# RWKV-7 scan rounds on TensorE: waits on constants, turns inside 64x64 tiles, and a new order of the steps

## The chip, the cores and the metric

One core of one Trainium2 chip runs the kernel. The metric is the device time of one execution in microseconds. PE is TensorE, DVE is VectorE, ACT is ScalarE, POOL is GpSimd.

## The reference, cut to what matters

The program is a network of several layers over 256 context and 256 latent tokens of width 1024, in fp32. One of them is an RWKV-7 layer with 16 heads of 64 channels, and the change is inside its recurrence. For each head and direction (context first, then the latent tokens from the context's last state):

```python
def step(S, inp):                       # S is 64 x 64 for each head
    rt, wt, kt, vt, kkt, at = inp
    sa = jnp.einsum("bhvk,bhk->bhv", S, -kkt)
    S = S * wt[:, :, None, :] + sa[..., None] * (kkt * at)[:, :, None, :] + vt[..., None] * kt[:, :, None, :]
    return S, jnp.einsum("bhvk,bhk->bhv", S, rt)
```

It runs once forwards and once backwards; the two outputs are added. Only the outputs of the latent tokens are used afterwards.

## The kernel before, in words

`rwkv_scan_stage` computes this in chunks of 64 tokens. Four chunks of context and four of latent tokens, for two sets of 8 heads, give 16 rounds for each direction. A direction is a **lane** (0 forwards, 1 backwards), and each round does both lanes. Rounds 0 to 7 are context (plain rounds below), rounds 8 to 15 are latent and also read out y (read rounds; `RW_READS` is 8). A tile of SBUF holds 128 partitions x 4 x 64 values: the two 64-partition halves carry different heads, so a product of two 64x64 blocks uses one quarter of the PE array, and eight of them make a step.

The steps of a round, for each lane:

- `grow`, `shrink` (ACT, L3367, L3371): the exponentials of the running decay; `last` (DVE, L3472) keeps its edge.
- `alpha`, `beta`, `kappa`, `rho` (POOL, L3414, L3419, L3435): the scaled keys and queries. `state`, `vn`, `ident`, `scale` are POOL's copies and scalings.
- `CT`, `LK`, `CC`: products of `alpha` with `beta`, `kappa`, and with `beta` and the state together (PE, L3241 and L3250). DVE masks them out of PSUM into `e1`, `lk` and `cw` (L3492, L3501, L3498).
- The inverse of a triangular 64x64 matrix, doubled in size level by level: for levels 2 to 6 the products `Y` and `E` (PE, L3258), with a transpose `D` of the inverse so far between them. ACT copies the results of `Y` and `D` from PSUM (L3384, L3391); DVE writes the result of `E` into `e` under a mask (`copy_predicated`, L3489). `Y2` needs `E6` of the round before and `CC`.
- `U`, `S`, `O` (PE, L3264, L3241): they apply the inverse of the round before, add to the state, and add to y. `V` and `KB` transpose `vn`, `kappa` and `beta` (L3269); ACT copies the three (L3375). `LKV` multiplies `lk` with the values.
- In read rounds also `RKB` (PE, two products of `rho` with `kappa` and `beta`; DVE masks both at once, L3507) and `R` (the state with `rho`; POOL adds it to y, L3442).

**Transposes.** `turn` transposes whole 128x128 blocks with PE's transpose (L3269), two for a step. In plain rounds `D` is a product with the identity instead (`turn_by_product`, eight 64x64 products, L3241); in read rounds it is `turn`.

**Order.** Every engine works through its own list, made by `rwkv_order(engine, n)`. A mark `+` means the step of round n+1, `'` that of round n-1. Nearly everywhere both lanes stand side by side, lane 0 first:

```python
return [*both("Y2", "D1", *["R"] * read, "U'"), *both("E2", *kept, *behind), *both("Y3", "D2"), *both("V", "KB"), *both("E3", "LKV"), *both("Y4", "D3", *reads), *both("E4"),
        *both("Y5", "D4"), *both("E5"), *lane(0, "Y6", "D5"), *fore[0], *lane(1, "Y6", "D5"), *fore[1], *both("E6")]
```

`fore[d]` is `CT+ CC+ LK+` of lane d. DVE's list ends with `fore[0]`, `fore[1]`, then E6 of both lanes, then `last+`.

**Waits.** The rounds of PE stand in two hardware loops, rounds 0 to 7 and rounds 8 to 14; round 15 and the rounds -1 and 16 (which hold only the steps ahead and behind) stand outside. The other engines' lists are written out in full. Each semaphore grows by one a round, so inside a loop PE waits for a value that is in a register:

```python
def wait(e, lane, step):
    pe.wait_ge(sig.sems[e, lane, step].sem, at)      # at is the loop's register
    if not isinstance(at, int):
        pe.sem_inc(carried.sem, 1)
```

Outside the loops `at` is a number. The other engines wait for PE by a count of its finished steps (`wait_pe`).

Of the kernel before, what the change touches and what calls it, by code (L numbers as in the profile page):

```python
# [3029 lines left out]

def rwkv_order(engine, n):

    late, read, more = n >= 1, n >= RW_READS, n + 1 < RW_ROUNDS
    inside = 0 <= n < RW_ROUNDS

    def lane(d, *steps):  # L3040
        at = {"'": n - 1, "+": n + 1}
        return [(d, s.rstrip("'+"), at.get(s[-1], n)) for s in steps]

    def both(*steps):
        return [x for d in LANES for x in lane(d, *steps)]

    fore = [lane(d, "CT+", "CC+", "LK+") if more else [] for d in LANES]
    reads, behind, kept = ["RKB"] * read, ["O'"] if n > RW_READS else [], ["S'"] if more else []
    if engine == "pe":
        if n < 0:  # L3050
            return fore[0] + fore[1]
        if read:
            behind = ["O'"]
        if not inside:
            return both("U'", *behind)
        return [*both("Y2", "D1", *["R"] * read, "U'"), *both("E2", *kept, *behind), *both("Y3", "D2"), *both("V", "KB"), *both("E3", "LKV"), *both("Y4", "D3", *reads), *both("E4"),
                *both("Y5", "D4"), *both("E5"), *lane(0, "Y6", "D5"), *fore[0], *lane(1, "Y6", "D5"), *fore[1], *both("E6")]
    if engine == "act":
        scales = both("shrink+", "grow+") if more else []
        if n < 0:  # L3060
            return scales
        behind = ["U'"]
        if not inside:
            return both(*behind)
        return [*both("Y2", "D1", *behind), *scales, *both("Y3", "D2"), *both("KB"), *both("Y4", "D3"), *both("Y5", "D4"), *both("Y6", "D5")]
    if engine == "dve":
        last = lane(0, "last+") + lane(1, "last+") if more else []
        if n < 0:
            return fore[0] + fore[1] + last
        if not inside:  # L3070
            return both(*behind)
        return [*both("copy"), *both("E2", *kept, *behind), *both("E3", "LKV"), *both(*reads), *both("E4"), *both("E5"), *fore[0], *fore[1], *both("E6"), *last]
    if n == RW_ROUNDS:
        return []
    ahead = [*both("ident+"), *both("alpha+"), *(both("scale'") if late and more else []), *both("state+", "vn+"), *both("beta+", "kappa+")] if more else []
    return [*ahead, *(both("rho+") if more and n + 1 >= RW_READS else []), *both(*["R"] * (read and inside))]


class ScanSignals:
# [3 lines left out]
    LAG = {"U": 1, "S": 1, "O": 1, "E6": 1, "kappa": -1}  # L3083
    STEPS = {"act": ("D1", "D2", "D3", "D4", "D5", "U", "KB", "grow", "shrink"),
             "dve": ("CC", "LK", "E2", "E3", "E4", "E5", "E6", "S", "O", "LKV", "RKB", "last", "copy"),
             "pool": ("alpha", "kappa", "rho", "scale", "R")}

    def __init__(self, core):
        self.sems = {(e, lane, s): core.counter(f"rw_{e}_{s}_{lane}") for e, steps in self.STEPS.items() for lane in LANES for s in steps}
        self.level = max(c.base for c in self.sems.values()) + 1  # L3090
        self.pe = [core.counter(f"rw_pe_steps_{lane}") for lane in LANES]
        self.pe_at, self.pe_n = {}, 0
        for n in range(-1, RW_ROUNDS + 1):
            for d, step, m in rwkv_order("pe", n):
                if d == 0:
                    self.pe_n += 1
                    self.pe_at[step, m] = self.pe_n

    def value(self, step, m):
        return self.level + m + 1 + self.LAG.get(step, 0)  # L3100

# [3 lines left out]
    def align(self, eng):  # L3105

        for (e, lane, s), c in self.sems.items():
            by = self.value(s, self.first(s) - 1) - c.base
            if by:
                eng.sem_inc(c.sem, by)  # L3110
# [2191 lines left out]
```

## Time and profile before

| what | value |
|---|---|
| median of 3 runs | 3288.19 us (3282.24 to 3291.73) |
| the profiled execution's own time | 3287.64 us |
| its span in the trace | 3285.9 us |
| PE, weight load, DVE, ACT, POOL busy | 93%, 76%, 72%, 53%, 19% |
| mean granted PE clock | 0.957 |
| start of Y2 of lane 0 in round 0, 8, 15 | 1065.70, 1207.68, 1372.91 us |

A row of the windows gives a stretch, then busy time and number of instructions for PE, weight loads, DVE, ACT and POOL, then the granted clock as a share of 2.4 GHz. A row of the timeline gives the start, the duration, the engine, the line and what is written from what; "xN" is how many instructions were merged, and a bracket is the idle time before it with what ended it. An fp32 product shows as two records, a transpose as one, so a step of eight 64x64 products is x16. Records of PE overlap: the next one starts long before the last one's recorded end, so its steps are counted from start to start.

### The profile page before, as it was taken

What the parts mean: (1) busy time and instruction counts of PE and PEld (TensorE: products, weight loads), DVE (VectorE), ACT (ScalarE), POOL (GpSimd) and SP (SyncE); (2) the same over time, 40 slices, a digit from 0 to 9 for tenths busy, and PEclk for the clock granted to TensorE, in tenths of its full rate; (3) what the DMA queues carried; (4) which work ended last, traced back from release to release, by engine and by line L of the source; (5) the groups of instructions that cost most, each with busy time, mean ns of one, the idle gap of its engine ahead of it and who ended that gap; (6) DMA issues with size and microseconds to landing.
All of it is one profiled execution on the core that took longest, in us unless ns stands there. A gap on an engine that the chain in (4) does not pass through costs nothing. (4 is left out here: it accounts for less than half of the span.)

```text
span 3285.9 us, 68297 instructions
## 1 busy us (share of the span) xinstructions
PE 3040.2 (93%) x27176; PEld 2492.1 (76%) x27176; DVE 2371.4 (72%) x3483; ACT 1743.1 (53%) x2797; POOL 615.4 (19%) x720
## 2 busy tenths in 40 slices
PE   5998889999797888879999999998999999999998
PEld 4774568878673777759986998866788888888887
DVE  5868754468847444477866778545799999999998
ACT  2424433232314443335445534765788888888887
POOL 0007124321100434318423111331000000000000
PEclk8998999999898999989989999998999999999999
DMA  6536224446211000048652798402899999999997
GB/s 221 170 108 20 103 84 153 141 147 207 96 58 26 1 1 1 2 171 271 253 161 65 275 328 302 140 27 79 320 370 367 371 369 366 373 366 368 370 360 261
DMA packets 337306, 646.56 MB, mean 197 GB/s; under 512 B 23853, under 2 KB 144281, under 8 KB 337113
## 3 DMA queue, kind: packets, MB, share of 16 engines
q1 hardware_dynamic: 316233, 568.38, 51.0%
q0 software_dynamic: 20160, 73.41, 6.1%
q8 instruction: 117, 1.92, 0.2%
q10 hardware_dynamic: 720, 2.23, 0.2%
q14 instruction: 76, 0.62, 0.1%
HBM read 641.34 MB, written 1.05 MB: 196 GB/s over the span
## 5 line engine op out<-in xcount | busy, mean ns | idle before, releaser
L5095 DVE TENSOR_TENSOR weights_lo<-raw_ring,weights_hi 128x1024 fp32r<-128x1024 f32 x336 | 400.8, 1220 | 35.6 <-ACT weights_hi L5025 28.4
L5025 ACT ACTIVATE weights_hi<-raw_ring 128x1024 fp32r<-128x1024 f32 x336 | 356.7, 1065 | 89.4 <-PE bank_pair L4961 53.2
L5095 DVE TENSOR_TENSOR weights_lo<-H,weights_hi 128x1024 fp32r<-128x1024 f32 x224 | 268.6, 1221 | 25.1 <-ACT weights_hi L5025 18.2
L4961 PE MATMUL bank_pair<-weights_hi,expert_x_hi 128*128 128x512 f32 x896 | 281.7, 396 | 4.9 <-DVE weights_lo L5095 4.8
L4961 PE MATMUL bank_pair<-weights_hi,expert_x_lo 128*128 128x512 f32 x896 | 277.2, 391 | 0.0
L4961 PE MATMUL bank_pair<-weights_lo,expert_x_hi 128*128 128x512 f32 x896 | 276.8, 390 | 0.0
L5025 ACT ACTIVATE weights_hi<-H 128x1024 fp32r<-128x1024 f32 x224 | 236.5, 1060 | 58.5 <-PE bank_pair L4961 43.2
L2715 DVE SCALAR_TENSOR_TENSOR conv<-bank_pair,vec,conv 128x189 f32<-128x189 f32 (+3 forms) x396 | 138.5, 427 | 146.0 <-ACT conv L2675 146.0
L4961 PEld LDWEIGHTS bank_pair<-weights_lo,expert_x_hi 128*128 128x128 f32 x896 | 168.5, 188 | 36.1
L4961 PEld LDWEIGHTS bank_pair<-weights_hi,expert_x_lo 128*128 128x128 f32 x896 | 168.5, 188 | 36.0
L4961 PEld LDWEIGHTS bank_pair<-weights_hi,expert_x_hi 128*128 128x128 f32 x896 | 163.8, 189 | 36.2 <-issue 5.1
L1349 PE MATMUL bank_pair<-Y_parts,const_parts 128*128 128x256 f32 (+1 forms) x592 | 145.7, 331 | 1.6 <-DVE H_parts L1394 1.6
L4973 PE MATMUL bank_pair<-weights_hi,hidden_hi 128*128 128x512 f32 x448 | 138.7, 391 | 0.0
L4973 PE MATMUL bank_pair<-weights_hi,hidden_lo 128*128 128x512 f32 x448 | 138.0, 389 | 0.0
L4973 PE MATMUL bank_pair<-weights_lo,hidden_hi 128*128 128x512 f32 x448 | 138.0, 389 | 0.0
L5095 DVE TENSOR_TENSOR weights_lo<-const,weights_hi 128x1024 fp32r<-128x1024 f32 x112 | 134.0, 1219 | 3.5
L5025 ACT ACTIVATE weights_hi<-const 128x1024 fp32r<-128x1024 f32 x112 | 119.4, 1066 | 31.9 <-PE bank_pair L4961 21.6
L629 DVE SCALAR_TENSOR_TENSOR mod_sums_ada<-mod_ring_ada,act,mod_sums_ada 128x1024 f32<-128x1024 f32 x84 | 115.4, 1379 | 4.8 <-DMA mod_ring_ada<-in_w_ada 4.8
L1349 PEld LDWEIGHTS bank_pair<-Y_parts,const_parts 128*128 128x128 f32 x592 | 101.9, 191 | 14.0 <-DVE const_parts L1329 2.4
L1138 PE MATMUL bank_pair<-const 128*128 128x512 f32 (+1 forms) x140 | 75.3, 649 | 32.2 <-PEq L214 32.2
L3384 ACT ACTIVATE const<-bank_pair 128x128 f32<-128x128 f32 x80 | 22.5, 282 | 150.3 <-PE bank_pair L3269 80.7
L1349 PE MATMUL bank_pair<-H_parts,const_parts 128*128 128x256 f32 (+1 forms) x296 | 97.7, 330 | 0.0
(802 smaller groups left out, 8366.9 us busy)
## 6 DMA issues: line engine op xcount, KB each, us to landing
raw_ring<-in_moe_w_gate SPq DMA_DIRECT2D x64, 1024.0 KB, 6.2
raw_ring<-in_moe_w_up SPq DMA_DIRECT2D x56, 1024.0 KB, 7.0
ring_up<-in_ffn_w_up SPq DMA_DIRECT2D x110, 512.0 KB, 4.0
H<-in_moe_w_down SPq DMA_DIRECT2D x48, 1024.0 KB, 5.1
raw_ring<-in_moe_w_down SPq DMA_DIRECT2D x48, 1024.0 KB, 5.1
mod_ring_ada<-in_w_ada POOLq DMA_DIRECT2D x84, 512.0 KB, 6.3
ring_down<-in_ffn_w_down SPq DMA_DIRECT2D x66, 512.0 KB, 6.0
H<-in_moe_w_gate SPq DMA_DIRECT2D x32, 1024.0 KB, 7.2
```

Source lines behind the costliest of these rows:

```text
L629: ins = self.core.nc.vector.scalar_tensor_tensor(total, tile, scale, total, ALU.mult, ALU.add)
L1138: core.nc.tensor.matmul(core.bank(bank)[:, cols], st.C("ones"), st.const[:, cols], start=True, stop=True)
L1349: ins = self.core.nc.tensor.matmul(self.bank(it, o)[:, 0:T], w, y, start=s == self.begin[o] and k == 0 and a == 0, stop=s == self.end[o] a ...
L2715: ins = nc.vector.scalar_tensor_tensor(out, shifted, tap(w, 2 * it + o), out, ALU.mult, ALU.add)
L3384: nc.scalar.activation(by_slot(t["y"])[:, :, :, 0:C // 2], Y[d], ACT.Copy)
L4961: ins = nc.tensor.matmul(bank, x[:, k * SEATS:(k + 1) * SEATS].bitcast(F32R), w[:, j * WIDE:(j + 1) * WIDE], start=k == 0 and i == 0, stop ...
L4973: ins = nc.tensor.matmul(DOWN[half], x, w[:, half * 512:(half + 1) * 512], start=c == 0 and i == 0, stop=c == FEC - 1 and i == 2)
L5025: nc.scalar.activation(hi[:, u % CUTS].bitcast(F32R), raw_part(u), ACT.Copy).then_inc(cut.sem, 1)
L5095: nc.vector.tensor_tensor(lo[:, u % CUTS].bitcast(F32R), raw_part(u), hi[:, u % CUTS], ALU.subtract).then_inc(parted.sem, 1)
```

## The change

It does four things. PE's waits inside the loops become waits on a constant: each producer raises a token by one, PE waits for one more than the base, and the second (and third) product of the step lowers it again. Only `V` still waits on the register. `D` in all rounds, and `V` and `KB` in plain rounds, are made inside the 64x64 tiles: four transposes and four products with the identity. `CT` and `LK` multiply by `alpha` and `rho` together (`keys`, 128 columns instead of 64) in every round; `RKB` goes, and DVE masks rho's halves in two operations, `RB` and `RK`, into `fresh`, and copies that to `rkb` (`cp`) once `O` of the round before is done. And the four lists are written out as tables in which the lanes are no longer side by side.

```diff
+RW_STEPS = {
+    ("pe", False): "Y20 D10 U0' Y21 D11 E20 U1' S0' E21 Y30 D20 S1' Y31 D21 V0 E30 V1 KB1 E31 Y40 D30 KB0 Y41 D31 LKV1 E40 LKV0 E41 CT1+ Y50 D40 Y51 D41 CT0+ E50 LK0+ E51 Y60 LK1+ D50 Y61 CC0+ D51 E60 CC1+ E61",
+    ("act", False): "grow0+ shrink0+ D10 grow1+ U0' D11 U1' D20 D21 shrink1+ KB1 D30 KB0 D31 D40 D41 D50 D51",
+    ("dve", False): "copy0 E20 copy1 E21 S0' S1' E30 E31 last0+ LKV1 last1+ E40 E41 LKV0 E50 CT0+ E51 LK0+ CT1+ LK1+ CC0+ E60 CC1+ E61",
+    ("pool", False): "ident1+ alpha1+ alpha0+ scale0' scale1' beta1+ kappa1+ ident0+ beta0+ kappa0+ vn0+ state0+ vn1+ state1+",
+    ("pe", True): "Y20 D10 R0 U0' Y21 D11 R1 U1' E20 E21 S0' O0' Y30 D20 Y31 D21 S1' O1' E31 E30 V0 KB0 V1 KB1 Y40 LKV0 D30 Y41 D31 LKV1 E40 E41 CT0+ LK0+ Y51 D41 Y50 D40 CT1+ E51 E50 LK1+ Y60 D50 CC0+ Y61 D51 E60 CC1+ E61",
+    ("act", True): "grow1+ grow0+ D10 shrink1+ U0' D11 shrink0+ U1' D20 D21 KB0 KB1 D30 D31 D41 D40 D50 D51",
+    ("dve", True): "copy0 copy1 E20 E21 O0' S0' O1' S1' E31 E30 LKV0 cp0 LKV1 E41 last1+ E40 cp1 CT0+ RB0+ LK0+ RK0+ E51 E50 CT1+ RB1+ LK1+ RK1+ CC0+ E60 last0+ CC1+ E61",
+    ("pool", True): "ident0+ rho0+ rho1+ alpha1+ ident1+ alpha0+ beta0+ scale1' scale0' kappa0+ beta1+ kappa1+ vn0+ state0+ vn1+ R0 R1 state1+",
+}
...
+    def take(self, eng, e, lane, step):
+
+        c = self.tokens[e, lane, step]
+        eng.wait_ge(c.sem, c.base + 1)
+        return c.sem
...
-            def turn_by_product(out, x):
-                return cross(out, [(x, ident)])
+            def turn(out, x):
+                for j in (0, 1):
+                    for s in (0, 1):
+                        for r in (0, 1):
+                            head, unit = x[HALF[r], 2 * j + s], st.C("pair_ident")[HALF[r]]
+                            if s:
+                                ins = nc.tensor.matmul(out[HALF[s], r, j], head, unit, start=True, stop=True)
+                            else:
+                                ins = nc.tensor.transpose(out[HALF[s], r, j], head, unit)
+                return ins
...
+                    def first(ins):
+                        count[0] += 1
+                        if count[0] > 1 and taken:
+                            ins.then_inc(taken.pop(0), -1)
+
                     if step == "CT":
-                        wait("pool", d, "kappa")
+                        take("pool", "kappa")
                         if n >= 0:
-                            wait("dve", d, "RKB" if n >= RW_READS else "LKV")
-                        ins = cross(SLOT0[d], [(t["beta"], t["alpha"])])
+                            take("dve", "LKV")
+                        ins = cross_both(WIDE0[d], t["beta"], t["keys"], first)
+                    elif step == "LK":
+                        ins = cross_both(WIDE1[d], t["kappa"], t["keys"], first)
...
-                        ins = (turn if n >= RW_READS else turn_by_product)(TURN[d], t["e1" if l == 1 else "e"])
+                        ins = turn(TURN[d], t["e1" if l == 1 else "e"])
...
-                        cross(SLOT0[d], [(t["kappa"], t["rho"])])
-                        ins = cross(SLOT1[d], [(t["beta"], t["rho"])])
...
+                        by = turn_whole if n >= RW_READS else turn
+                        by(SLOT0[d], t["kappa"])
+                        ins = by(SLOT1[d], t["beta"])
...
-                for name in ("e", "w", "ur", "turned"):
+                for name in ("e", "w", "ur", "turned", "rho"):
...
+                    elif step in ("RB", "RK"):
+                        mask = st.C(f"upto_{d}").unsqueeze(1).unsqueeze(1).to_broadcast([P, 2, 2, C])
+                        if m > RW_READS:
+                            sig.wait(dve, "dve", d, "cp", m - 1)
+                        wide_slot, i = (WIDE0, 1) if step == "RB" else (WIDE1, 0)
+                        ins = nc.vector.tensor_tensor(by_slot(t["fresh"][:, i]), wide_slot[d][:, :, :, 1], mask, ALU.mult)
+                    elif step == "cp":
+                        ins = nc.vector.tensor_copy(t["rkb"], t["fresh"])
```

`turn_whole` is the old `turn`. In each table word the digit before the mark is the lane. Some of the waits of ACT and POOL now name another step of PE (`grow` and `shrink` wait for `CT`, `beta` and `kappa` for `KB`, `rho` for `R`).

## Rows read from the trace of the kernel before

**Rows 1.** The page: its first line and PE's busy time.

```profile
span 3285.9 us, 68297 instructions
PE 3040.2 (93%) x27176; PEld 2492.1 (76%) x27176; DVE 2371.4 (72%) x3483; ACT 1743.1 (53%) x2797; POOL 615.4 (19%) x720
```

**Rows 2.** Windows by round and by group of rounds, columns as described above.

```profile
1065.70:1088.05 22.35, 16.45 (x728) 14.86 (x721) 9.73 (x30) 8.03 (x28) 6.13 (x12) 1.00 0.01 4
...
1122.25:1139.33 17.08, 14.94 (x717) 14.03 (x717) 8.14 (x25) 8.07 (x28) 7.19 (x14) 1.00 0.00 0
...
1207.68:1237.20 29.52, 24.61 (x736) 21.34 (x737) 9.36 (x26) 8.71 (x28) 9.94 (x18) 0.77 0.01 3
...
1282.02:1303.72 21.70, 19.19 (x737) 16.81 (x737) 10.05 (x29) 8.67 (x28) 9.89 (x18) 1.00 0.00 1
...
1065.70:1207.68 141.98, 121.01 (x5741) 113.04 (x5733) 66.72 (x198) 64.43 (x224) 57.81 (x112) 1.00 0.00 1
1207.68:1372.91 165.23, 145.52 (x5152) 127.15 (x5153) 69.32 (x192) 60.75 (x196) 69.34 (x126) 0.92 0.00 1
1372.91:1395.10 22.19, 19.17 (x672) 16.22 (x672) 7.75 (x23) 8.20 (x26) 1.46 (x2) 1.00 0.02 4
```

**Rows 3.** Timeline of plain round 3: level 5, then its last steps.

```profile
1132.04 0.43 PE L3258 MATMUL bank_pair<-const,cw 64*64 64x32 f32 x16
...
1132.96 0.30 ACT L3391 ACTIVATE const<-bank_pair 128x128 f32<-128x128 f32 x1
...
1133.40 0.43 PE L3258 MATMUL bank_pair<-const 64*64 64x32 f32 x16 [0.20 <-ACT const L3391]
...
1133.90 0.33 DVE L3489 COPY_PREDICATED const<-const,bank_pair 128x128 f32<-128x128 uint32 x1 [1.64 <-PE bank_pair L3258]
...
1134.38 0.43 PE L3258 MATMUL bank_pair<-const,cw 64*64 64x32 f32 x16
...
1134.60 0.47 PE L3241 MATMUL bank_pair<-const 64*64 64x64 f32 x16
...
1134.86 0.44 PE L3241 MATMUL bank_pair<-const,H 64*64 64x64 f32 x16
...
1135.10 0.65 PE L3250 MATMUL bank_pair<-H,const 64*64 64x128 f32 x16
...
1135.54 0.44 PE L3241 MATMUL bank_pair<-const 64*64 64x64 f32 x16
...
1137.79 0.68 DVE L3498 COPY cw<-bank_pair 128x512 f32<-128x512 f32 x1
...
1138.72 0.30 DVE L3489 COPY_PREDICATED const<-const,bank_pair 128x128 f32<-128x128 uint32 x1
...
1139.33 0.43 PE L3258 MATMUL bank_pair<-const,cw 64*64 64x32 f32 x16 [1.49 <-DVE const L3489]
```

**Rows 4.** Timeline of read round 11, PE alone: its start, then V, KB and E3.

```profile
1282.02 0.43 PE L3258 MATMUL bank_pair<-const,cw 64*64 64x32 f32 x16 [1.50 <-DVE const L3489]
1282.39 0.44 PE L3269 MATMUL bank_pair<-const 128*128 128x128 f32 x2
1282.76 0.68 PE L3264 MATMUL bank_pair<-const,H 64*64 64x64 f32 x16
1283.28 0.57 PE L3264 MATMUL bank_pair<-const 64*64 64x64 f32 x13
...
1289.04 0.60 PE L3269 MATMUL bank_pair<-const 128*128 128x128 f32 x4
...
1290.45 0.43 PE L3258 MATMUL bank_pair<-const 64*64 64x32 f32 x16
```

**Rows 5.** Timeline of round 15, which waits on constants: the end of level 5.

```profile
1388.17 0.33 DVE L3489 COPY_PREDICATED const<-const,bank_pair 128x128 f32<-128x128 uint32 x1 [1.89 <-PE bank_pair L3258]
...
1388.56 0.43 PE L3258 MATMUL bank_pair<-const,cw 64*64 64x32 f32 x16
```

**Rows 6.** Groups by line around the scan: mask of RKB, count, busy us, mean ns.

```profile
L3507 DVE TENSOR_TENSOR H<-bank_pair,const 128x512 f32<-128x512 f32 x16 | 11.1, 691 | 12.2 <-PE bank_pair L3241 12.2
```

More of the change, by code:

```diff
@@ L3028 @@
 LANES = (0, 1)
-def rwkv_order(engine, n):
[L3037 to L3076, printed above, removed]
@@ new lines @@
+RW_STEPS = {
[8 rows of a table added]
+}
+def rwkv_order(engine, n):
+    read, more = n >= RW_READS, n + 1 < RW_ROUNDS
+    steps = []
+    for word in RW_STEPS[engine, read].split():
+        step, d, at = step_of(word)
+        ahead, behind = at == "+", at == "'"
+        if (ahead and not more) or (not ahead and n < 0) or (not behind and n == RW_ROUNDS):
+            continue
+        if (step == "S" and not more) or (step == "scale" and not (n >= 1 and more)) or (step == "O" and engine == "dve" and n == RW_READS):
+            continue
+        first_read = n == RW_READS - 1
+        if first_read and engine == "pool" and step == "kappa":
+            steps.append((d, "rho", n + 1))
+        steps.append((d, step, n + ahead - behind))
+        if first_read and engine == "dve" and step in ("CT", "LK"):
+            steps.append((d, "RB" if step == "CT" else "RK", n + 1))
+    return steps
@@ L3079, with step_of @@
+def step_of(word):
+    at = word[-1] if word[-1] in "+'" else ""
+    word = word.rstrip("+'")
+    return word[:-1], int(word[-1]), at
 class ScanSignals:
[L3083 to L3086, printed above, removed]
+    STEPS = {"act": ("grow", "shrink"), "dve": ("S", "O", "last", "copy", "CT", "cp"), "pool": ("scale", "R")}
+    TOKENS = {"act": ("D1", "D2", "D3", "D4", "D5", "U", "KB"), "dve": ("E2", "E3", "E4", "E5", "E6", "LKV", "LK", "CC"), "pool": ("kappa", "state")}
@@ new lines, in __init__, with wait_pe, value @@
+                self.pe_at[d, step, m] = self.pe_n[d]
+    def align(self, eng):
+        for lane in LANES:
+            c = self.sems["dve", lane, "S"]
+            eng.sem_inc(c.sem, self.level - c.base)
+            c.n += self.level - c.base
+            eng.sem_inc(self.tokens["dve", lane, "E6"].sem, 1)
+    def wait_pe(self, eng, lane, step, m):
+        eng.wait_ge(self.pe[lane].sem, self.pe[lane].at(self.pe_at[lane, step, m]))
+    def value(self, e, lane, step, m):
+        if step == "S":
+            return self.level + m + 2
+        first = RW_READS if step in ("O", "R", "cp") else 0
+        return self.sems[e, lane, step].at(m + 1 - first)
@@ L3232, in _, with cross @@
         def _(pe):
[L3233 to L3235 removed]
+            def cross(out, products, first=lambda ins: None):
                 for j in (0, 1):
```

181 lines of the change are left out of this document (81 added, 100 removed).

## The prediction

> **What bounds the kernel now.** The page comes first: one core, a span of 3285.9 us, TensorE (PE) 93% busy over the whole [rows 1]. That average says nothing about the change, which touches one stage. The windows by stage [rows 2] are the second view. The scan runs from 1065.7 to 1395.1 us, a tenth of the span. Rounds 0 to 7 take 141.98 us, rounds 8 to 14 (which also read out y) 165.23 us, the last round and its tail 22.19 us. A plain round is 17.08 us with PE busy 14.94; a read round is 21.70 us with PE busy 19.19. DVE is busy 8 to 10 us of a round, ACT 8 to 9, POOL 7 to 10. So no engine is full: a round is a chain of handoffs laid over much PE work.
>
> The timeline shows which. A middle level of a plain round goes Y product, turn (D), ACT copy, E product, DVE write, and the next Y starts 2.34 us later (1132.04 to 1134.38) [rows 3]. Two steps of it are pure handoff: ACT ends at 1133.26, PE starts at 1133.40; DVE ends at 1134.23, PE starts at 1134.38, so 0.14 and 0.15 us. At the round's end DVE works through CT, CC and LK of both lanes before E6 of lane 0: its copy CC starts at 1137.79, E6 only at 1138.72, and Y2 of the next round at 1139.33, 0.31 us after E6 ended, with PE idle 1.49 us [rows 3].
>
> In the read rounds the turn is a 128x128 transpose between 64x64 products. Y takes 0.37 us until the turn starts, against 0.22 in a plain round, and the turn another 0.37 until the next product [rows 3, 4].
>
> **The change, part by part.**
>
> *Waits on constants.* The last round already waits on constants, since it stands outside the loops: DVE ends at 1388.50, Y6 starts at 1388.56, so 0.06 us against 0.15 [rows 3, 5]. That is 0.09 us for each late handoff, ten on a lane's chain, plus the second wait ahead of Y2 (0.31 to 0.06). A level becomes 2.34 - 2 x 0.09 = 2.16 us, five of them 10.8: the chain of one lane is then well under the round. The tokens are taken back by decrements on the second and third product of a step. No row shows such a decrement; it rides on an instruction that is there anyway, so 0 from below. From above it can cost no more than the time between two groups of products, some 0.06 us (16 records in 0.22 to 0.24 us, four at a time) at some 34 waits, 2 us a round. I take 0, nearest to the increments that end every step today. The Trainium skill ("TensorE: Matmul & The Clock Gate", the cost of the per-tile semaphore tail) has each further increment at a tail of tiles add 26 ns to it; by that estimate up to 0.9 us a round would come on top, if the decrements counted the same. No run here shows it.
>
> *PE issue of a plain round.* Start to start, from the rows: Y or E 0.22, D 0.26, CT or LK 0.24, CC 0.44 [rows 3]; a step on its own diagonal 0.52 before another such (R to U) [rows 4] and, as an estimate, 0.40 before a Y, which may begin on the free tiles; S, with twice D's records, 0.50; V and KB of both lanes 1.41 plus 0.15 to enter [rows 4]. Sum now: 20 x 0.22 + 10 x 0.26 + 4 x 0.24 + 2 x 0.44 + 2 x 0.50 + 4 x 0.40 + 1.56 = 13.0 us. After: CT and LK are made for alpha and rho together, also in plain rounds, where nobody reads rho's half. They cost CC's 0.44: + 4 x 0.20. The turn inside the tiles has four transposes and four products: the column half that does the products has as many records as now, so D stays at 0.26, and the six turns of V and KB become 1.56. Sum 13.8 us.
>
> *PE issue of a read round.* Now 20 x 0.22 + 10 x 0.52 + 2 x 0.52 + 2 x 0.40 + 4 x 0.50 (S, O) + 2 x 0.50 (RKB) + 1.56 + 2 x 0.40 + 4 x 0.24 + 2 x 0.44 = 18.6 us. After: D falls from 0.52 to 0.26 (-2.6), RKB goes (-1.0), CT and LK widen (+0.8): 15.8 us. V and KB stay whole here.
>
> *DVE and the others.* A read round gains RB and RK for both lanes, each half of RKB's 0.69 [rows 6] from below and all of it from above (twice the width); I take 0.4. It gains cp twice, between E's masked write (0.33) and CC's copy of the same size out of PSUM (0.68) [rows 3]; I take 0.5. RKB's 2 x 0.69 go. That is +1.2 us on 10.05 [rows 2], under the round. POOL keeps its operations, 9.89 us. Neither binds in sum; only place matters.
>
> *The order.* I walked one round of each kind through the four new lists with these prices. In a plain round CT of lane 1 is queued as soon as its LKV is read, four steps before level 5 ends; CC of both lanes stands after D5. DVE has only CC of lane 0 (0.68) ahead of E6 of lane 0, not six operations. PE is then late at four places: E61 for ACT's last copy (0.15 us), E20 (0.05), E41 and Y20 (under 0.1), and at the loop's end. The branch's own cost is in no row: 0 from below, 1.49 us (the idle that covers it today [rows 3]) from above; I take 0.3, since so far the whole of it lies in that idle and the waits behind it are met by DVE. Round: 13.8 + 0.3 + 0.2 = 14.3 us. In the read round: LKV0 waits for ACT's copy of KB (0.1), E41 for D3 (0.2), Y60 for DVE, which has cp, CT, RB, LK and RK ahead of E50 (0.2), E61 and Y20 as above: 15.8 + 0.3 + 0.8 = 16.9 us. The cover that could go: kappa of lane 0 on POOL is due only 0.5 us before CT wants it in a read round, and everything behind CT on PE would wait with it. In the plain round the same margin is about 1 us.
>
> *Sum.* Plain rounds 8 x (17.08 - 14.3) = 22.2. Round 0 takes 22.35 us at full clock for the same work [rows 2]; its extra 5.3 stays. Read rounds 7 x (21.70 - 16.9) = 33.6. The last round has constants already; it gains ten turns of 0.26 and RKB, some 3.5 us in all. The opening round -1 with wider CT and LK, and two more memsets, -0.5.
>
> *Clock.* The seven read rounds take 165.23 - 7 x 21.70 = 13.3 us more than seven at full clock. The granted clock over them is 0.92, in round 8 0.77 (29.52 us); in the plain rounds it is 1.00 [rows 2]. So some 26 of 165 us ran at 1.2 instead of 2.4 GHz. PE had stood idle or between array sizes at the round's end. From below nothing comes back, from above all 13.3; I take 5. The same page of the Trainium skill (PE-mode transpose) says that transposes do not count as busy for the clock: by it the read rounds' turns would explain the falls (the trace agrees, the plain rounds use products and hold 1.00), and the new turns, a third transposes in plain rounds too, speak for a rival below.
>
> Sum: 22.2 + 33.6 + 3.5 - 0.5 + 5 = 63.8 us off the profiled execution's 3287.64, which stands 0.6 under the median of 3288.19 (runs 3282 to 3292). Forecast 3224 us.
>
> **The rivals.**
> 1. *The new order waits where the walk sees none.* Only the handoffs and half of the turns' gain come through: plain 17.08 - 1.05 = 16.0, read 21.70 - 1.05 - 1.8 = 18.9, last round 2 us. 8 x 1.05 + 7 x 2.85 + 2 = 30, so 3257 us. For it: the thin margin of kappa; against it: DVE, ACT and POOL are under 12 us of a round.
> 2. *The clock falls in plain rounds as it does in read rounds*, and nothing comes back there. The same share at 1.2 GHz (16% of 114 us, 18 us), at 13.3 / 26 = 0.5 us lost for each, costs 9, and the 5 go: 3238 us. Against it: PE has fewer gaps than today.
> 3. *Slower: a turn that mixes transposes and products drains the array at each change.* The one such change in the trace costs 0.15 us in (0.37 - 0.22) and 0.15 out (0.37 less two transposes at 0.11) [rows 3, 4]; whether size or kind of operation causes it, no row tells. The new turn has two groups of transposes, so 0.60 us at the full price. A plain round has 16 turns: 14.3 + 9.6 = 23.9; a read round 10: 22.9. That gives 8 x 6.8 + 7 x 1.2 + 2.5 more than now, 3353 us; at half the price 3291. It decides at 0.28 us a turn (the 58.8 us gained without the clock, over 8 x 16 + 8 x 10 = 208 turns). Against it: the transposes stay in the same tile grid. The Trainium skill ("TensorEngine Tiling (Array Packing)", Key Properties) has a drain for a change of tiling mode alone, which speaks against this rival (the trace's 0.15 agrees); the same page (Feature Incompatibilities) has column tiling exclude transposes of fp32, which speaks for it.
>
> **How the numbers follow.** Forecast 0.62, rival 1 0.20, rival 2 0.08, rival 3 0.07, nothing measurable 0.03. The forecast's own range is 3208 (all 13 us of the clock back, no waits) to 3242 (decrements at 2 us a round in a third of the rounds, a branch of 1 us). To hold eight in ten it reaches over rivals 2 and 1: 3208 to 3262. A measurement of this kernel can tell about 0.3% from no change, 3278 to 3298: faster 0.89, same 0.04, slower 0.07.
>
> **What would show it.** Y2 to Y2 of lane 0 at 14.3 us in plain and 16.9 in read rounds; ACT or DVE end to PE start at 0.06; Y to turn at 0.22 in read rounds, no 128x128 transposes but V and KB there; PE's idle at the round's end under 0.5 us. Wrong would be: turns longer than 0.4 us, a granted clock under 1.00 in plain rounds, or DVE writing E6 later than PE is free.

## The result, and the profile after

The kernel after takes **3350.04 us** (median of 4 runs, 3347.91 to 3357.34), the kernel before beside it 3289.96 us (4 runs, 3282.24 to 3295.8). The ratio is 1.0188, with a 95% interval of 1.0161 to 1.0215: **slower by 1.9%**. The forecast was 3224 us and its range ended at 3262, so the prediction was wrong. Its third rival, at a chance of 0.07, had said 3353 us.

The page of the kernel after, first line and busy times, beside [rows 1]:

```profile
span 3346.1 us, 68801 instructions
PE 3133.7 (94%) x27624; PEld 2552.6 (76%) x27624; DVE 2388.5 (71%) x3517; ACT 1744.9 (52%) x2797; POOL 613.1 (18%) x720
```

PE has 448 records more and is busy 93.5 us longer. DVE is busy 17 us longer. The windows of the kernel after, with the columns of [rows 2], are: one plain round, one read round, rounds 0 to 7, rounds 8 to 14, the last round with its tail.

```profile
1141.84:1166.22 24.38, 24.18 (x737) 19.71 (x737) 8.49 (x25) 8.24 (x28) 7.05 (x14) 1.00 0.00 0
1335.32:1358.38 23.06, 22.87 (x772) 19.74 (x773) 11.73 (x33) 8.72 (x28) 10.08 (x18) 1.00 0.00 1
1067.07:1265.37 198.30, 196.59 (x5888) 160.75 (x5889) 69.65 (x196) 65.90 (x224) 56.45 (x112) 0.98 0.00 1
1265.37:1427.37 162.00, 160.31 (x5405) 138.31 (x5405) 81.55 (x223) 60.37 (x194) 70.57 (x126) 1.00 0.00 1
1427.37:1454.10 26.73, 25.24 (x712) 21.42 (x708) 7.08 (x21) 8.22 (x26) 1.46 (x2) 0.82 0.01 3
```

A plain round went from 17.08 to 24.38 us and a read round from 21.70 to 23.06. PE is now busy 24.18 of 24.38 us: **the gaps of the chain are gone, and PE itself is the bound**. The number of its records per round rose only from 717 to 737, so about the same number of records takes much longer to pass. Counted from the starts: the scan begins 1.4 us later, rounds 0 to 7 take 56.3 us more (198.30 - 141.98), rounds 8 to 14 take 3.2 less (162.00 - 165.23), the tail 4.5 more. That makes 59.0 of the 60.2 us by which the span grew.

The timeline of the kernel after, plain round 3, from Y2 of lane 0 through one turn; L3281 is a transpose, L3279 a product with the identity:

```profile
1141.84 0.43 PE L3257 MATMUL bank_pair<-const,cw 64*64 64x32 f32 x16 [0.20 <-issue]
...
1142.21 0.24 PE L3281 MATMUL bank_pair<-const 64*64 64x64 f32 x2
...
1142.38 0.33 PE L3279 MATMUL bank_pair<-const 64*64 64x64 f32 x4
...
1142.64 0.25 PE L3281 MATMUL bank_pair<-const 64*64 64x64 f32 x2
...
1142.82 0.28 PE L3279 MATMUL bank_pair<-const 64*64 64x64 f32 x2
```

Start to start, Y to the first transposes is 0.37 us (a turn by products followed Y after 0.22 [rows 3]), two transposes to the products behind them 0.17, two products (four records) to the next transposes 0.26, transposes to products 0.18. In the kernel before, sixteen records of products passed in 0.22 to 0.26 us [rows 3]; here two transposes alone hold up the products behind them for 0.17. That points at the changes of kind, although all of it stays in the 64x64 grid; e1 and e2 test it. The last steps of a plain round of the kernel after, PE alone:

```profile
1165.59 0.43 PE L3257 MATMUL bank_pair<-Y 64*64 64x32 f32 x16
1166.22 0.43 PE L3257 MATMUL bank_pair<-const,cw 64*64 64x32 f32 x16 [0.20 <-issue]
```

E6 of lane 1 starts 0.63 us before the next Y2, and PE idles 0.20 us, with nothing named but issue, where it idled 1.49 us for DVE [rows 3]. That alone does not show that the order and the constant waits work as forecast: a PE that needs 10 us more for a round would cover such waits too. e1, e4 and e12 show it.

### The profile page after: what moved, and what is told of

It reads as the page before. It is cut to its first block and busy times, and to the rows that moved or that the text cites. A ratio compares the mean times of both kernels' runs of the same rounds, so it can differ in the third digit from the quotient of the medians.

```text
span 3346.1 us, 68801 instructions
## 1 busy us (share of the span) xinstructions
PE 3133.7 (94%) x27624; PEld 2552.6 (76%) x27624; DVE 2388.5 (71%) x3517; ACT 1744.9 (52%) x2797; POOL 613.1 (18%) x720
## 3 DMA queue, kind: packets, MB, share of 16 engines
HBM read 641.34 MB, written 1.05 MB: 192 GB/s over the span
## 5 line engine op out<-in xcount | busy, mean ns | idle before, releaser
L4985 PEld LDWEIGHTS bank_pair<-weights_lo,hidden_hi 128*128 128x128 f32 x448 | 84.1, 188 | 17.6
```

The lines of the kernel that those rows point to most:

```text
L4985: ins = nc.tensor.matmul(DOWN[half], x, w[:, half * 512:(half + 1) * 512], start=c == 0 and i == 0, stop=c == FEC - 1 and i == 2)
```

## The experiments

Each ran beside the kernel before on the same chip, whose medians were 3285.5 to 3286.9 us. "Products" are fp32 products of 64x64 blocks, two records each. The length of a loop's body is given as its "product records": PE's records of a round without the weight loads, the transposes counted in.

### e1: all turns inside the tiles by products

```diff
-                            if s:
-                                ins = nc.tensor.matmul(out[HALF[s], r, j], head, unit, start=True, stop=True)
-                            else:
-                                ins = nc.tensor.transpose(out[HALF[s], r, j], head, unit)
+                            ins = nc.tensor.matmul(out[HALF[s], r, j], head, unit, start=True, stop=True)
```

> The kernel after with every turn inside the tiles made of eight products with the identity, no transposes (128x128 transposes stay where they were, in V and KB of read rounds). Theory M (mixing transposes and products in one turn is the whole loss): a mixed turn now takes 0.77 to 0.86 us start to start where a turn by products took 0.26, so about 0.55 us goes for each; plain rounds fall from 24.4 to about 15.1 us, read rounds from 23.07 to about 17.5, the kernel from 3350 to about 3232 us. Rival O (the new order, the wide CT and LK or the decrements cost something too): plain rounds stay over 17 us and read rounds over 20, the kernel at 3280 us or more.

Measured: 3271.19 us, ratio 0.9956 (0.9939 to 0.9973). Its windows, a plain round, then a read round, and three stretches of 2 us at that read round's end:

```profile
1114.24:1128.63 14.39, 14.20 (x801) 13.95 (x801) 8.51 (x25) 7.91 (x28) 6.97 (x14) 1.00 0.00 1
1210.03:1231.22 21.19, 16.75 (x819) 16.05 (x816) 12.10 (x34) 8.69 (x28) 10.14 (x18) 0.97 0.01 2
1226.00:1228.00 2.00, 0.78 (x32) 0.57 (x27) 1.44 (x5) 1.01 (x4) 0.00 (x0) 1.00 0.09 16
1228.00:1230.00 2.00, 0.00 (x0) 0.00 (x0) 0.00 (x0) 0.00 (x0) 0.00 (x0) 1.00 0.00 0
1230.00:1232.00 2.00, 0.78 (x19) 0.71 (x19) 0.00 (x0) 0.00 (x0) 0.00 (x0) 0.52 0.03 8
```

The plain rounds are settled: more records (800 instead of 736) in 14.39 us instead of 24.38. The mixed turn costs (24.38 - 14.39) / 16 = **0.62 us more** than one by products. The forecast's 14.3 us for the rest of a plain round was right. PE's idle at the round's end is 0.19 us here, with nothing that covers it; the timeline of PE, kernel e1, the next plain round's Y2:

```profile
1128.63 0.43 PE L3257 MATMUL bank_pair<-const,cw 64*64 64x32 f32 x16 [0.19 <-issue]
```

The read rounds show **something no theory had**. Every engine stands still for some 4 us at the loop's end, PE waits for "issue" and not for a semaphore, and only a few small transfers run. After it the clock is at 0.52. Over the stage, such gaps of PE (4.7 to 5.2 us from start to start) come at every second branch back, one of 2.2 to 2.5 us close behind each, and several of about 1 us further on in the round. The timeline of PE there, kernel e1:

```profile
1226.34 0.43 PE L3257 MATMUL bank_pair<-Y 64*64 64x32 f32 x16
1231.22 0.65 PE L3257 MATMUL bank_pair<-const,cw 64*64 64x32 f32 x16 [4.45 <-issue]
1231.65 0.45 PE L3278 MATMUL bank_pair<-const 64*64 64x64 f32 x3
1234.27 0.59 PE L3278 MATMUL bank_pair<-const 64*64 64x64 f32 x11 [2.17 <-issue]
```

The new theory (L): a loop body of more than some 800 product records is fetched anew in each iteration. The plain body has 800 records, the read body 812.

### e2: four transposes, then four products

```diff
-                for j in (0, 1):
-                    for s in (0, 1):
+                for s in (0, 1):
+                    for j in (0, 1):
```

> The kernel after with the same four transposes and four products in each turn, but the four transposes first: one change from transposes to products and one back for each turn instead of two and two. Theory M1 (the price is for each change of kind): a turn falls from 0.77 to about 0.5 us, plain rounds from 24.4 to about 20, read rounds from 23.07 to about 20.3, the kernel from 3350 to about 3292 us. Rival M2 (the price is for each 64x64 transpose, or for the turn as a whole): all as in the kernel after, 3350 us.

Measured: 3292.84 us, ratio 1.0023 (1.0013 to 1.0033). Windows of e2, a plain and a read round:

```profile
1145.68:1165.82 20.14, 19.94 (x737) 17.25 (x737) 8.48 (x25) 8.25 (x28) 7.01 (x14) 1.00 0.00 0
1289.47:1309.87 20.40, 20.21 (x772) 18.20 (x773) 11.62 (x33) 8.72 (x28) 10.05 (x18) 1.00 0.00 1
```

The same records, in two groups instead of four: 4.24 us less in a plain round with 16 turns (0.27 a turn), 2.66 less in a read round with 10 (0.27 a turn). The groups that are left cost (20.14 - 14.39) / 16 = 0.36 a turn. The price goes by the number of changes; the number of transposes has little part in it. The timeline of PE, kernel e2, one turn:

```profile
1142.54 0.30 PE L3281 MATMUL bank_pair<-const 64*64 64x64 f32 x4
1142.77 0.28 PE L3279 MATMUL bank_pair<-const 64*64 64x64 f32 x2
```

Four transposes in a row hold the products behind them back 0.23 us, where two held them back 0.17.

### e3: the mixed turn alone, in the kernel before

```diff
             def turn_by_product(out, x):
-                return cross(out, [(x, ident)])
+                ... the mixed turn of the change, line for line
```

> The kernel before with one thing of the change: D of the plain rounds as four transposes and four products instead of eight products. Theory M: ten turns a round cost 0.51 to 0.6 us more each, plain rounds go from 17.08 to 22 or 23 us, read rounds stay at 21.7, the kernel goes from 3290 to about 3331 us or more. Rival O (the turn is harmless, the order or the waits are the cause): 3290 us.

Measured: 3343.15 us, ratio 1.0169 (1.0152 to 1.0186). The windows of two plain rounds of e3, the second the only one at full clock:

```profile
1134.84:1158.73 23.89, 21.55 (x676) 18.43 (x677) 8.23 (x25) 8.16 (x28) 7.25 (x14) 0.93 0.00 0
1236.06:1258.57 22.51, 20.17 (x677) 17.23 (x677) 8.14 (x25) 8.06 (x28) 8.54 (x16) 1.00 0.00 1
```

Without the new order, the wide products or the constants, the mixed turn alone takes a plain round from 17.08 to 23.89 us. It has ten turns of the kind, 0.68 us each, a part of which is the lower clock (0.93). At full clock it is (22.51 - 17.08) / 10 = 0.54 a turn. This one edit costs 56 us. That is near the 60 us that the whole change loses, but not the same sum: the change has sixteen such turns in a plain round and ten in a read round, and its other parts win much of that back.

### e4: the constant waits alone, in the kernel before

```diff
-                            wait("dve", d, f"E{l - 1}")
+                        take("dve", "E6" if l == 2 else f"E{l - 1}")
...
-                        wait("act", d, f"D{l - 1}")
+                        take("act", f"D{l - 1}")
```

and so for U, KB, LK, LKV and RKB; V, CC and the waits for POOL's steps still use the register. POOL's R waits for PE's O now, instead of ACT's U.

> The kernel before, its order and its turns, with PE's waits for E, D, U, KB, LK, LKV and RKB on constants and taken back by a decrement; kappa, rho, CC, S and O keep the register, and CC is waited for ahead of E6. Theory W (0.09 us for each late handoff, decrements free): plain rounds 17.08 to about 16.0 us, read rounds 21.70 to about 20.7, the kernel from 3290 to about 3274 us. Rival D (decrements cost what the constants save): rounds within 0.2 us of before, 3290 us, or slower.

Measured: 3267.54 us, ratio 0.9934 (0.9912 to 0.9956). Windows of e4, a plain and a read round, then a handoff of its level 5:

```profile
1134.01:1150.37 16.36, 14.77 (x717) 13.70 (x717) 8.17 (x25) 8.02 (x28) 7.20 (x14) 1.00 0.00 0
1242.84:1264.01 21.17, 19.10 (x736) 16.68 (x736) 10.04 (x29) 8.66 (x28) 9.89 (x18) 1.00 0.00 0
```

```profile
1145.32 0.33 DVE L3511 COPY_PREDICATED const<-const,bank_pair 128x128 f32<-128x128 uint32 x1 [1.48 <-PE bank_pair L3270]
1145.70 0.44 PE L3270 MATMUL bank_pair<-const,cw 64*64 64x32 f32 x16
```

DVE ends at 1145.65 and PE starts at 1145.70, 0.05 us against 0.15 in the kernel before. A round gains 0.72 us in plain and 0.53 in read rounds, where ten handoffs of 0.09 and the one at the round's end would be 1.05. So half to two thirds of it shows, with CC's wait ahead of Y2 still on the register.

The medians differ by 19.4 us, twice what the rounds give (8 x 0.72 + 7 x 0.53 = 9.5). In the two traces the rest lies mostly in rounds 8 to 14, which take 165.23 us at a clock of 0.92 in [rows 2]. In e4:

```profile
1199.45:1350.29 150.84, 135.51 (x5153) 118.26 (x5153) 69.75 (x196) 60.65 (x196) 69.35 (x126) 0.99 0.00 1
```

### e5 and e6: a shorter read body

e5 is e1 with D of levels 4 and 5 in read rounds as whole 128x128 transposes (756 product records in the body), e6 with level 5 alone (784). A whole turn leaves its blocks of `d` in another order than a turn by products. From level 2 on ACT writes only half the columns of `d`, so where the kind of turn changes between levels (here and in e9) the two orders mix, and the read rounds compute other values with the same amount of work.

```diff
+WHOLE_LEVELS = (4, 5)
...
+def whole_at(n, l):
+    return n >= RW_READS and l in WHOLE_LEVELS
...
-                        ins = turn(TURN[d], t["e1" if l == 1 else "e"])
+                        ins = (turn_whole if whole_at(n, l) else turn)(TURN[d], t["e1" if l == 1 else "e"])
```

> e1_products with D4 and D5 of the read rounds as whole 128x128 transposes (as in the kernel before). e1_products had plain rounds of 14.4 us, but read rounds of 21.2 to 25.3 us in which all engines stand still for 4 to 5 us at the loop's end. Theory L (the read loop's body, 812 product records a round, is too long to be kept, and is fetched anew each time round; plain rounds with 800 are kept): at 756 records the stand-still goes, read rounds are 16.5 us of work plus 4 turns at 0.25 us, about 17.6 us, the kernel about 3231 us. Rival T (it comes from the tokens or the order of the read rounds): read rounds stay over 21 us, the kernel at 3271 us.

> As e5_whole45 with D5 alone whole in the read rounds, 784 product records a round. Theory L: below the 800 that plain rounds keep, so no stand-still, read rounds about 17.1 us, the kernel about 3228 us. If the limit is not in records but moves with something else, the stand-still stays and the kernel is near 3270 us.

Measured: e5 3230.05 us, 0.9826 (0.9805 to 0.9846); e6 3232.8 us, 0.9836 (0.9817 to 0.9856). A read round of each:

```profile
1248.17:1265.85 17.68, 17.55 (x756) 16.18 (x757) 11.25 (x33) 8.64 (x29) 10.15 (x18) 1.00 0.00 1
```

```profile
1262.65:1279.95 17.30, 17.16 (x785) 16.15 (x785) 11.38 (x33) 8.69 (x29) 10.13 (x18) 1.00 0.00 0
```

No stand-still, though turns were made dearer. A whole turn costs (17.68 - 17.30) / 2 = 0.19 us more than one by products; what it removes cost 4 to 8 us a round.

### e7 and e9: bodies made longer

e7 is the kernel before with D by products in its read rounds too, 876 records in that body. It tries the limit without the change's order, waits or wide products.

```diff
-                        ins = (turn if n >= RW_READS else turn_by_product)(TURN[d], t["e1" if l == 1 else "e"])
+                        ins = turn_by_product(TURN[d], t["e1" if l == 1 else "e"])
```

> The kernel before with D by products in the read rounds too: each turn 0.26 instead of 0.51 us, but 876 product records a round instead of 736. Theory L: each read round from the second on stands still for 4 to 5 us at the loop's end, 21.7 - 2.6 + 4.7 = about 23.8 us, and the clock falls more often, the kernel at 3300 us or more. Rival (length does not matter): read rounds about 19.3 us, the kernel about 3270 us.

Measured: 3332.68 us, 1.0131 (1.0095 to 1.0166). A plain and a read round of e7:

```profile
1136.00:1153.10 17.10, 14.96 (x716) 14.04 (x717) 8.14 (x25) 8.05 (x28) 7.20 (x14) 1.00 0.00 0
1257.71:1292.07 34.36, 24.23 (x876) 22.81 (x877) 10.10 (x28) 8.68 (x28) 10.00 (x18) 0.80 0.02 4
```

D by products, the cheaper form of the two in plain rounds, makes this kernel 47 us slower. From round 9 on its read rounds take 22.5 to 35.6 us where 19.3 were expected without a stand-still, most of them at a clock of 0.76 to 0.80. So the length of the body is enough, without the change's order, waits or wide products. e9 is e5 with V of the plain rounds made twice, so that their body grows from 800 to 832 records.

> e5_whole45 with the turn V of the plain rounds made twice (the second writes the same values again): 832 product records a plain round instead of 800, read rounds unchanged. Theory L: the plain rounds now stand still too, from 14.4 to about 19.5 us, the kernel about 35 us over e5_whole45. Rival T: plain rounds grow by the two turns alone, to 14.9 us, the kernel by 4 us.

Measured: 3283.28 us against e5's 3230.05, 53 us for 32 records a round. Two plain rounds of e9, which take 14.4 us in e5:

```profile
1134.58:1154.03 19.45, 14.67 (x832) 14.42 (x833) 8.63 (x25) 7.89 (x28) 6.97 (x14) 1.00 0.01 2
1154.03:1179.03 25.00, 18.49 (x832) 17.61 (x833) 8.38 (x24) 8.11 (x28) 7.05 (x14) 0.87 0.02 5
```

### e10: whole turns at all levels of the read rounds

The layout of `d` follows the turn here as it does in the kernel before, so all values are those of the change. 672 records in the read body.

```diff
-                        ins = turn(TURN[d], t["e1" if l == 1 else "e"])
+                        ins = (turn_whole if n >= RW_READS else turn)(TURN[d], t["e1" if l == 1 else "e"])
```

> The kernel after, with the turns of the plain rounds all by products (as in e1) and D of the read rounds, all five levels, as whole 128x128 transposes, as before. The body of the read loop has 672 product records. Theory (a body over about 800 records stands still once an iteration, nothing else is wrong with read rounds): no stand-still, and a whole turn costs what e5 and e6 show between them, (17.68 - 17.29) = 0.39 us a level, so read rounds of 17.68 + 3 x 0.39 = 18.9 us, plain rounds 14.4, and with e5's 3230 a time of 3230 + 8 x 1.2 = 3239 us (3232 to 3248). Rival (short turns were needed for the read rounds' order to work, whole turns wait on each other as before): read rounds of 21 us or more, 3255 us or more.

Measured: 3240.67 us, 0.9855 (0.9834 to 0.9875). Windows of e10, rounds 0 to 7, rounds 8 to 14, then one read round:

```profile
1066.97:1189.82 122.85, 115.18 (x6400) 112.37 (x6401) 69.26 (x196) 63.37 (x224) 56.07 (x112) 1.00 0.00 1
1189.82:1324.97 135.15, 133.48 (x4710) 114.96 (x4705) 80.08 (x223) 60.76 (x194) 70.61 (x126) 1.00 0.00 1
1229.32:1248.53 19.21, 19.03 (x673) 16.39 (x673) 11.55 (x33) 8.79 (x29) 10.09 (x18) 1.00 0.00 0
```

Against [rows 2] the plain rounds give 19.1 us and the read rounds 30.1. Of these, 7 x (21.70 - 19.2) = 17.5 are the rounds' own, and the 13.3 us lost to the clock come back nearly whole: the granted clock over the read rounds is 1.00 where it was 0.92, **with D by whole transposes as before**.

### e11: a body just under 800

```diff
-                        ins = turn(TURN[d], t["e1" if l == 1 else "e"])
+                        ins = (turn_grouped if n >= RW_READS and l >= 4 else turn)(TURN[d], t["e1" if l == 1 else "e"])
```

`turn_grouped` is the turn of e2.

> The same as e1, with D of levels 4 and 5 in the read rounds as four transposes and then four products: every value is laid out as in e1, and the body of the read loop has 812 - 16 = 796 product records. Theory (the limit of the body lies between 800 and 812 records): no stand-still, read rounds of 16.9 + 4 x 0.36 = 18.3 us, plain 14.4, time 3241 us (3233 to 3250). Rival A (the limit lies between 784 and 796 where there is other work in the loop): the stand-still of e1 stays, read rounds of 22 to 25 us, 3270 us or more. Rival B (the price of a change of kind was paid by plain rounds only): read rounds of 17, 3231 us.

Measured: 3282.31 us (10 runs, from 3270.06 to 3298.64), 0.9994 (0.9971 to 1.0017). The stand-still is back at 796 records, while the plain body of 800 in the same kernel has none. My theory's number was wrong: the limit is not one count of records for both loops. Windows of e11, a plain round, a read round with gaps, and round 14, which has none:

```profile
1115.01:1129.43 14.42, 14.22 (x800) 13.95 (x801) 8.53 (x25) 7.92 (x28) 6.99 (x14) 1.00 0.00 1
1240.40:1262.87 22.47, 18.11 (x796) 16.89 (x797) 11.81 (x34) 8.61 (x28) 10.15 (x18) 0.96 0.01 1
1336.83:1354.92 18.09, 18.09 (x796) 16.90 (x797) 11.17 (x33) 7.97 (x26) 10.15 (x18) 1.00 0.01 1
```

Round 14 takes 18.09 us, near the 18.3 expected. So the two turns a lane cost what was said, and the rest goes with the stand-still and the clock after it.

### e12: the old order in plain rounds

e12 is e10 with the plain rounds' lists of PE, DVE and ACT side by side again. It is not wholly the old order: CT and LK stand ahead of Y6, where the kernel before has them, with CC, behind it.

```diff
-    ("pe", False): "Y20 D10 U0' Y21 D11 E20 U1' S0' E21 Y30 D20 S1' ...
+    ("pe", False): "Y20 D10 U0' Y21 D11 U1' E20 S0' E21 S1' Y30 D20 Y31 D21 V0 KB0 V1 KB1 E30 LKV0 E31 LKV1 ...
```

> The same as e10, with the plain rounds' steps in the order of the kernel before on TensorE, VectorE and ScalarE (both lanes side by side, lane 0 first). Theory (the order is worth what e4 left over: with constants, products and the old order a plain round took 16.36 us, in the new order 14.4): plain rounds of 16 to 16.8 us, time 3239 + 8 x 2 = 3255 us (3249 to 3262). Rival (the plain rounds are bound by what TensorE issues, and the order adds nothing): plain rounds of 14.4 to 14.8 us, and the time of e10 within 4 us.

Measured: 3248.64 us, 0.988 (0.9856 to 0.9903). A plain round of e12:

```profile
1116.15:1131.86 15.71, 15.19 (x801) 14.38 (x801) 8.33 (x25) 7.93 (x28) 6.98 (x14) 1.00 0.00 1
```

This part of the order is worth 15.71 - 14.42 = 1.3 us a plain round, and 8.0 us of the medians: between the two expectations, nearer to the first.

### e14: level 5 whole, in the products' layout

```diff
-                        ins = turn(TURN[d], t["e1" if l == 1 else "e"])
+                        ins = (turn_whole if n >= RW_READS and l == 5 else turn)(TURN[d], t["e1" if l == 1 else "e"])
...
-                            if l > 1:
+                            if n >= RW_READS and l == 5:
+                                to = t["d"].rearrange("p (r j) t -> p j r t", r=2)
+                            elif l > 1:
```

> The kernel after, with all turns by products but D of level 5 in the read rounds, which is a whole 128x128 transpose laid out as the products lay it (ScalarE copies all 256 columns of it, 0.10 us more than half of them by the rows of e1: 380 ns against 280). The body of the read loop has 784 product records, between e5 (756, no stand-still) and e11 (796, stand-still); all values are those of the kernel after. Theory: no stand-still (the page's instruction queue at 118 as in e6, not 146), read rounds of 17.3 to 17.6 us, plain 14.4, a time of 3234 us (3228 to 3242), the best of the series. Rival (e6 was short because of what its altered layout left out): the stand-still is back, read rounds over 20 us, 3262 us or more.

Measured: **3233.63 us** (5 runs, 3229.49 to 3245.39), 0.9838 (0.9824 to 0.9853), the fastest of the kernels that compute all that the kernel before computes. The profiled execution was the slowest of the five, and shows why. Windows of e14, a read round in the third place of the loop, then a later one:

```profile
1231.11:1257.03 25.92, 21.34 (x785) 19.66 (x785) 11.28 (x31) 8.98 (x28) 10.10 (x18) 0.83 0.02 4
1274.44:1291.85 17.41, 17.20 (x784) 16.14 (x785) 11.37 (x33) 8.89 (x29) 10.15 (x18) 1.00 0.00 0
```

The first three read rounds took 22.0, 22.2 and 25.9 us and the later ones 17.2 to 17.4. The first is no sign of the edge, since it takes 22.0 us in e6 too; the second and third are. A body of 784 records stands at the edge.

**The instruction queue.** The DMA view of the page lists a queue of instruction packets of 16 KB. It points to the cause without any timing. Its row for rounds 9 to 14 of e1, then for rounds 9 and 10 of e14, then for rounds 1 to 6 of e9:

```profile
q8 instruction: 27, 0.44, 1.5%
```

```profile
q8 instruction: 9, 0.15, 1.5%
```

```profile
q8 instruction: 27, 0.44, 1.6%
```

That is 27 / 6 and 9 / 2 = 4.5 packets a round in all three. The plain rounds of e1 (800 records), the read rounds of e5 (756) and e10 (672) and rounds 11 to 14 of e14, beyond the first round of each loop, have no row for this queue (e10 has one packet more as round 9 begins). Over the whole kernel the page counts 117 packets before, 119 after, 118 in e5, e6, e10 and e12, 127 in e14, 145 to 147 in e1, e9 and e11, and 155 in e7. The Trainium skill ("Runtime: NRT & Kernel Launch", Instruction fetch mechanics) has PE's instruction memory hold 2048 instructions, refilled in blocks of 256 and 16 KiB, and a taken branch out of the window that is held, two such blocks, wait for a fetch. The packets' size agrees. The window does not: the bodies of e10 and of e1's plain rounds, 1355 and 1611 instructions by the same count as below, branch back without a fetch. By its 2048 the 1603 instructions of e11's body (796 loads, 796 products, 11 others in the trace) would fit, and they did not; if whole blocks count, an estimate from that page is that a body may lie over seven blocks or eight according to where it begins. If only seven could stay, 800 records could fit in one loop and 796 fail in the other. No run here moves the start of a loop whose body is at this edge, so that stays open.

## Why the prediction was wrong

**The step that failed** is in the part on PE's issue of a plain round: "the column half that does the products has as many records as now, so D stays at 0.26, and the six turns of V and KB become 1.56". It priced the turn by its records and left out what lies between them. Measured, a mixed turn costs 0.62 us on top of one by products (e1), and 0.54 at full clock in the kernel before (e3). Over 16 turns that is 10 us of a plain round; the same term made the read rounds 23.06 instead of 16.9. Rival 3 had the mechanism and the price: 0.60 us a turn, plain rounds 23.9 (24.38 measured), read rounds 22.9 (23.06), 3353 us (3350). That the totals agree within 3 us is in part luck: it had rounds 8 to 14 8.4 us longer, and they are 3.2 shorter, because the clock came back there; the plain rounds, the last round and the scan's start took more than it had, and make up for about half of that. The point from which it decides, 0.28 us a turn, was near: at e2's 0.36 the kernel stands 5.9 us behind the kernel before, which over the same 208 turns puts the point at 0.33.

Two arguments had pushed the rival to 0.07. "The transposes stay in the same tile grid" was the chief one. The only change in the trace of before altered size and kind together, and I gave all of its 0.15 us to the size [rows 3, 4]. e1 and e2 show that kind alone suffices. Neither row had spoken for one or the other, so the two halves deserved like chances. The other was the rule of the Trainium skill ("TensorEngine Tiling (Array Packing)", Key Properties) that a change of tiling mode drains the engine. It says nothing against other drains, and I read it as though it did; the runs show a delay of 0.14 us or more a change inside a single mode (0.27 for two in e2).

Point by point:

- **Handoffs, 0.09 us each:** right (0.05 against 0.15 in e4). Their sum of 1.05 us a round came to 0.72 and 0.53.
- **Decrements at 0:** right within what can be told. With some 34 of them a round, e1's plain round is 14.39 us against the walk's 14.3, which leaves no room for the upper bound of 2 us, if the walk's other terms hold as they seem to. By the 26 ns each of the Trainium skill ("TensorE: Matmul & The Clock Gate", the cost of the per-tile semaphore tail) it would have been 15.2.
- **Plain round without the turn's price, 14.3:** right (14.39 in e1). The part of the order that e12 takes back is worth 1.3 us.
- **DVE +1.2 us in read rounds:** 11.73 against 10.05, so +1.7; of no effect, since DVE is far under the round. CC of both lanes no longer holds up E6: PE's idle at the round's end fell from 1.49 to 0.19 in e1, near the 0.3 taken for the branch.
- **Read round 16.9:** right as far as can be told, apart from the turns. e6 gives 17.30 with one level of five as whole turns, which cost 2 x 0.19. No run shows all ten turns cheap: by products the body has 812 records, and rounds take 21.2 to 25.8 (e1). The change's own body is not concerned. Its mixed turn has 12 records where one by products has 16, so its read rounds have 772, and its rounds 9 to 14 show no fetch. The limit came in only with the cure by products, and no term of the forecast held it.
- **Round 0, 5.3 us kept as a constant:** not a constant. The row was there, 22.35 us at full clock beside 17.08 [rows 2], and I did not ask what PE waits for when a loop's body is new to it. Round 0 fetches five or six instruction packets in each of these kernels (five in the kernel before, then one in the seven rounds after it). It takes 20.98 us in e1, where later ones take 14.4, but 20.17 in e2 and 24.44 in the kernel after, no longer than their later ones. A round that is itself slower than the fetch hides it. Windows of round 0, kernel after, then e1:

```profile
1067.07:1091.51 24.44, 24.18 (x737) 19.71 (x737) 8.80 (x24) 8.23 (x28) 5.86 (x12) 1.00 0.02 4
```

```profile
1064.41:1085.39 20.98, 15.24 (x800) 14.41 (x801) 8.83 (x24) 8.02 (x28) 5.82 (x12) 1.00 0.02 5
```

- **Clock, 5 of 13.3 us back:** too low. In the kernel after the read rounds hold 1.00, and in e10 too. The rule that transposes do not count as busy for the clock (the Trainium skill, "TensorE: Matmul & The Clock Gate", PE-mode transpose) would have whole transposes pull it down; e10 has them in every read round at 1.00, so here the trace disagrees. In e1, e7, e9 and e14 a fall follows a PE that stood still for microseconds. The mixed turns go with falls in plain rounds, which the prediction had named as a sign of being wrong: e3 is at 0.91 over its plain rounds, and the kernel after has two of eight (2 and 6) at 0.93, 25.95 us each, while e2 holds 1.00. What sets off the falls in the read rounds of the kernel before, which fetch nothing after the first, is not shown. e4 keeps its order and its whole transposes, changes only waits, and has 0.99 there, in one trace.
- **Rivals 1 and 2:** neither happened, but for the two plain rounds at 0.93. Where the turn is cheap PE is busy 17.16 of 17.30 us in a read round (e6), so no wait of the order, kappa's among them, is left to be found.

The sum of what came true: without the mixed turn, and with a read body that fits, the change is worth 3233.63 against 3286.19 us, 1.6%. That is 53 of the 64 us forecast.

## What to carry to other kernels

Price a step on TensorE by its changes of kind as well as by its records: transposes put between products cost about 0.15 us at each change, even in the same tile grid, so a turn of 64x64 blocks among products is best made by products alone, or its transposes kept together. Count the instructions of a hardware loop's body before adding any, and look at the instruction queue in the page's DMA part: if its packets grow with the iterations, a round pays for it, mostly 4 to 11 us here with the clock that falls after it, and a dearer step with fewer instructions is the faster one. And where the only sample of a price changed two things at once, give both explanations a fair chance.

## What the hardware showed that was not expected

- A change between transposes and products in one 64x64 grid costs 0.14 to 0.18 us (0.54 to 0.62 for the four of a turn in e3 and e1, 0.27 for two and 0.36 for the other two in e2): two transposes hold the next products back 0.17 us, two products (four records) the next transposes 0.26 (timeline of after); two changes fewer a turn give back 0.27 us (e2).
- A PE loop with a body of 800 product records runs without fetches in plain rounds. In read rounds 672 to 772 do, 784 does after one to three iterations, and 796, 812 and 876 do not; 832 does not in plain rounds. Where it does not, rounds are 4 to 9 us longer in e1, e11 and e14, 5 to 11 in e9 and 3 to 16 in e7, lower clock included. PE has gaps of 4.4 to 5.4 us at every second branch back (in e7 at three in a row); the other engines run out of work behind it, and a lower clock can follow (0.52 right after it in e1).
- The first iteration of such a loop fetches five or six packets of 16 KB and takes 19 to 22 us where the later ones take 14 to 17 (round 0 of the kernel before, e1, e4, e10 and e12).
- e11 and e14 vary with it from run to run: 3270 to 3299 us and 3229 to 3245 us.
- A PE wait on a constant starts 0.05 us after its producer ends, one on a register 0.15 us after it.
